# Picking the experts' input rows with products on TensorE instead of a store and indirect gathers

## The reference, cut to what matters

```python
glog = h @ w_rg + b_rg;  gprob = softmax(glog);  g_idx = argmax(glog);  g_w = max(gprob)     # 4 groups
elog = h @ w_re + b_re                                                                       # 8 experts per group
ev, ei = top_k(elog[g_idx], 2);  ew = softmax(ev)                                            # 2 of 8
combine[expert] = g_w * ew                                                                   # zero for all others
y += sum_e  (silu(h @ w_gate[e]) * (h @ w_up[e]) * combine[e]) @ w_down[e]                   # 32 experts
```

## Time and profile before

| | us |
|---|---|
| three runs | 734.08, 734.78, 737.99 |
| median | 734.78 |
| profiled execution: span from first to last instruction | 733.4 |
| its own time | not listed apart; the median is 1.4 over the span |

### The profile page before, as it was taken

One profiled execution on the slowest core, in us unless ns is written; L12 is line 12 of the kernel. 1 busy time (PEld: TensorE's weight loads), 2 busy tenths in 40 slices (PEclk: granted clock), 3 DMA queues, 4 the chain that ended last, 5 costly groups with the idle time before them and its releaser, 6 DMA issues.

```text
span 733.4 us, 13507 instructions
## 1 busy us (share of the span) xinstructions
PE 637.2 (87%) x4935; PEld 450.3 (61%) x4935; DVE 281.4 (38%) x1551; ACT 149.3 (20%) x425; POOL 103.4 (14%) x137
## 2 busy tenths in 40 slices
PE   6999999799999989999998999638997995768674
PEld 4888888687888767743535877436653554444431
DVE  3003845988878976400000222535233221110103
ACT  3333323233326222200010000211100110101013
POOL 1456206320100324000000000011100110000001
PEclk9999999999999999999999999858998998999996
DMA  9938997999998999769999699668999999999871
GB/s 308 291 116 296 365 370 251 328 352 381 348 337 311 391 351 363 301 246 349 410 409 360 224 423 388 266 214 311 351 391 402 372 389 397 388 390 416 365 264 61
DMA packets 94901, 242.86 MB, mean 331 GB/s; under 512 B 8834, under 2 KB 54530, under 8 KB 86514
## 3 DMA queue, kind: packets, MB, share of 16 engines
q1 hardware_dynamic: 58050, 193.51, 69.9%
q10 hardware_dynamic: 31200, 31.39, 12.9%
q0 software_dynamic: 5584, 17.08, 6.9%
HBM read 234.88 MB, written 9.11 MB: 333 GB/s over the span
## 4 chain that ended last, share of the span: by engine, by line
PE 65%; DMA 19%; DVE 9%; SPq 3%; issue 2%; ACT 1%; ACTq 0%; DVEq 0%; POOLq 0%
PE zps L913 40%; PE nps L1195 5%; PE nps L1071 4%; DMA ring_all<-in_w_up 3%; DMA headT<-in_w_up 3%; DMA kall<-in_w_up 3%; DVE kall L1385 3%; DMA ring_all<-in_w_ret_o 3%; PE zps L1218 2%; DMA zret<-in_w_up 2%; PE nps L884 2%; DMA hT<-in_w_down 2%; PE zps L884 1%; PE zps L1184 1%; SPq L453 1%
## 5 line engine op out<-in xcount | busy, mean ns | idle before, releaser
L913 PE MATMUL zps<-hT,ring_all 128*128 128x264 f32 x1152 | 273.5, 393 | 1.6 <-DVE hT L1564 1.0
L913 PEld LDWEIGHTS zps<-hT,ring_all 128*128 128x128 f32 x1152 | 217.6, 193 | 44.9 <-issue 4.2
L1385 DVE CUSTOM_DVE_ANT_0 kall<-kall,qb 128x128 f32<-128x128 f32 x512 | 129.2, 318 | 62.5 <-DMA kall<-in_cache_k 60.0
L606 POOL DMA_INDIRECT rows_b<-h_rows,tidx_i x16 | 15.0, 938 | 343.7 <-DVEq L1652 193.5
L913 PE MATMUL zps<-headT,ring_all 128*128 128x264 f32 x256 | 58.5, 388 | 3.6 <-DMA ring_all<-in_w_ret_o 2.2
L913 PEld LDWEIGHTS zps<-headT,ring_all 128*128 128x128 f32 x256 | 48.2, 190 | 14.7 <-issue 4.8
L1071 PE MATMUL nps<-ring_all,zret 128*64 128x512 f32 x224 | 51.5, 599 | 2.6 <-DMA ring_all<-in_cache_v 2.6
L1726 DVE TENSOR_TENSOR qdT<-qdT,nps 128x64 f32<-128x64 f32 x32 | 7.1, 221 | 101.7 <-ACT qdT L820 101.2
L1385 DVE DVE_READ_ACCUMULATOR2_ANT scores<- 128x1 f32 x512 | 40.5, 79 | 0.0
L1551 DVE TENSOR_TENSOR hT<-zps,zatt 128x264 f32<-128x264 f32 x8 | 3.5, 432 | 92.7 <-PE zps L913 92.6
L820 ACT ACTIVATE qdT<-nps 128x64 f32<-128x64 f32 x32 | 7.1, 223 | 144.5 <-PE nps L1195 144.5
(11 more groups left out here) (374 smaller groups left out, 805.8 us busy)
## 6 DMA issues: line engine op xcount, KB each, us to landing
kall<-in_cache_k SPq DMA_DIRECT2D x64, 512.0 KB, 6.7
ring_all<-in_cache_v SPq DMA_DIRECT2D x56, 512.0 KB, 7.7
ring_all<-in_w_in ACTq DMA_DIRECT2D x26, 1024.0 KB, 9.7
ring_all<-in_w_gate SPq DMA_DIRECT2D x10, 1024.0 KB, 21.5
ring_all<-in_w_up SPq DMA_DIRECT2D x10, 1024.0 KB, 24.4
ring_all<-in_w_down SPq DMA_DIRECT2D x8, 1024.0 KB, 12.7
ring_all<-in_w_in SPq DMA_DIRECT2D x6, 1024.0 KB, 13.4
kall<-in_w_gate SPq DMA_DIRECT2D x5, 1024.0 KB, 16.9
```

Source lines behind the costliest of these rows:

```text
L606: pool.indirect_dma_start(out=rows, out_offset=None, in_=h2_rows, in_offset=bass.IndirectOffsetOnAxis(ap=col, axis=0), bounds_check=T - 1, ...
L913: mm = pe.matmul(zps[m % 2][:, 0:T], w[:, k, P * fb:P * (fb + 1)], rhs[:, k, :], start=(k == 0), stop=(k == KT - 1))
L1385: ins = v.tensor_tensor_reduce(kh, kh, qb[b % 2][:, P * h:P * (h + 1)], 1.0, 0.0, ALU.mult, ALU.add, scores[:, pg, AH * b + h:AH * b + h + 1])
```

## The change

The rows of a quad (4 experts, 128 slots) are now picked by products. DVE builds `chosen`, for each of the three row tiles a matrix tokens x 128 slots that holds the token's inverse root where the token has the slot and 0 elsewhere (`choose`, two instructions of 128x384). TensorE multiplies, for each of 8 feature blocks and each of 3 row tiles, the residual rows `xs[0:r, t, k:DM:KT]` (weights, every eighth column) with `chosen` (128 columns moving), adding up over the row tiles. A quad has two halves of 4 blocks, 12 products each; `quad_x_copy` takes each half with the gain into `xgT`, which now holds a whole quad. The store of `h2_rows`, the row table, the index conversion, the gathers and the transposes are gone. The residual of the samples, which grows during the stage, is moved to a copy on partitions 32 to 39, because `xs` must stay as it was.

```diff
-            sp.wait_ge(h2_out, 48)
+            sp.wait_ge(h2_root, 1)
             down_in(5, 5)
@@ GpSimd
-            pool.wait_ge(h2_out, 48)
-            pool.wait_ge(t_idx, 1)
-            def gather(par, rows, col):
-                pool.indirect_dma_start(out=rows, out_offset=None, in_=h2_rows,
...
-            for p in range(NPAIR):
-                if p >= 2:
-                    pool.wait_ge(e_T, p - 1)
-                gather(p % 2, xg[p % 2], tidx_i[0:2 * CAP, p:p + 1])
@@ ScalarE
-            for t, r in enumerate(ROWS):
-                link(act.activation(h2n[t][0:r, :], xs[0:r, t, :], ACT.Copy, scale=st[0:r, 9 + t:10 + t]))
-                act.dma_start(h2_rows[P * t:P * t + r, :], h2n[t][0:r, :]).then_inc(h2_out, 16)
+            copy(ysam, xs[0:NB, 2, :]).then_inc(y_kept, 1)
@@ TensorE
-            pe.wait_ge(t_lhs, 2)
-            row_table(bps[:, 768:768 + NE], onA, onB)
+            def chosen_rows(out, k, slots):
+                for t, r in enumerate(ROWS):
+                    mm = pe.matmul(out, xs[0:r, t, k:DM:KT], chosen[0:r, t, 0:slots], start=(t == 0), stop=(t == 2))
+                return mm
+            def quad_x(bank, q, half):
+                pe.wait_ge(e_chosen, q + 1)
+                for k in range(HK):
+                    mm = chosen_rows(bank[:, P * k:P * (k + 1)], HK * half + k, P)
+                mm.then_inc(e_T, 1)
+            for half in range(2):
+                quad_x(zps[half], 0, half)
...
+            def next_quad_x(q, half):
+                pe.wait_ge(e_Tc, 2 * q + half)
+                if q >= 2 or half == 1:
+                    pe.wait_ge(e_pickTc, q - 1 + half)
+                quad_x(zps[0], q, half)
...
             for e in range(NE):
                 expert_gate_up(e)
-                if e % 2 == 0 and e // 2 + 1 < NPAIR:
-                    pair_x(e // 2 + 1)
+                if e % 2 == 1 and e // 4 + 1 < NQUAD:
+                    next_quad_x(e // 4 + 1, e % 4 // 2)
                 if e >= 5 and e % 4 in (1, 2):
                     quad_down(e // 4 - 1, e % 4 - 1)
                 h_tr(e % 2, e + 1)
...
-                if e == 4:
-                    tile_rows()
@@ VectorE
+            def choose(q, pos):
+                if q >= 1:
+                    v.wait_ge(e_T, 2 * q)
+                out = chosen[:, :, :].rearrange("p t (e c) -> p t e c", e=4)
+                link(at_slots(out, q, pos))
+                v.tensor_tensor(out, out, rE[:, :, 4 * q:4 * (q + 1)].unsqueeze(3).to_broadcast([P, 3, 4, CAP]),
+                                ALU.mult).then_inc(e_chosen, 1)
             v.wait_ge(t_pos, 1)
...
+            choose(0, mps[:, 0:3 * NE].rearrange("p (t e) -> p t e", t=3))
...
-            x_copy(0, 1, 2 * CAP)
+            for half in range(2):
+                quad_x_copy(zps[half], 0, half)
+            token_weights()
+            v.wait_ge(y_kept, 1)
             for e in range(NE):
                 hidden(e % 2, e + 1)
-                if e % 2 == 0 and e // 2 + 1 < NPAIR:
-                    x_copy((e // 2 + 1) % 2, e // 2 + 2, 2 * CAP)
-                if e == 0:
-                    token_weights()
+                if e // 4 + 1 < NQUAD:
+                    if e % 4 == 0:
+                        choose(e // 4 + 1, posE)
+                    if e % 2 == 1:
+                        quad_x_copy(zps[0], e // 4 + 1, e % 4 // 2)
                 if e % 4 == 1:
                     pick_rows(e // 4)
...
-                if e == 5:
-                    tile_rows()
```

More of the change, by code:

```diff
@@ L39 @@
 TILES = P // CAP
-NPAIR = NE // 2
+HK = KT // 2
 NQUAD = NE // 4
@@ L56 @@
            ("kdec", RH), ("rope", 2 * T), ("diag", NB * NB), ("own", AH), ("spread", NB * AH), ("edge", EDGES), ("slot", CAP),
-           ("order", NE), ("val", 6), ("tile", XT), ("before", 16), ("after", 16)]
+           ("order", NE), ("tile", XT), ("before", 16), ("after", 16)]
 COL, _at = {}, 0
@@ L264, in build @@
         v_soon = [kall[:, 0:2048], kall[:, 2048:4096], zdec_all[:, 0:2048], zdec_all[:, 2048:4096]]
-        xg = [rows_b[2 * CAP * i:2 * CAP * (i + 1), :] for i in range(2)]
         ysb = rows_a
+        at_s = slice(32, 32 + NB)
+        ysam = xs[at_s, 2, :]
         scores_f = scores[:, :, :].rearrange("p a b -> p (a b)")
@@ L275, in build @@
             down_w[i] = ring[(g + 2) % RING]
-        xgT = [gain[:, 512 * i:512 * (i + 1)] for i in range(2)]
+        xgT = [buf[:, :].rearrange("p (k s) -> p k s", k=KT) for buf in (gain, rows_b)]
+        chosen = sb("chosen", [P, 3, P])
         acT = [scores_f[:, 256 * i:256 * (i + 1)] for i in range(2)]
@@ L871, in _ @@
             act.wait_ge(f_gained, 1)
-            act.activation(fsam, fbuf[1][0:NB, :], ACT.Copy, scale=st[0:NB, 11:12]).then_inc(o_x[2], 1)
+            act.activation(fsam, fbuf[1][at_s, :], ACT.Copy, scale=st[at_s, 11:12]).then_inc(o_x[2], 1)
             act.wait_ge(o_x[2], 1)
@@ L1164, in tile_base @@
             def tile_base():
[L1165 removed]
+                pe.wait_ge(t_lhs, 2)
                 pe.matmul(mps[:, 640:640 + NE], xcnt_b, upper[0:NE, 0:NE], start=True, stop=True)
                 pe.matmul(mps[:, 704:705], xcnt_b, ones[0:NE, 0:1], start=True, stop=True).then_inc(t_pos, 1)
[L1169 to L1185 removed]
             def gate_up(par, x, b, x_copied, landed):
@@ L1236, in sample_rows @@
             def sample_rows(bank, q, half, rows):
-                pe.matmul(bank[0:NB, :], pickT[q % 2][0:rows, S:T], ysb[0:rows, 512 * half:512 * (half + 1)],
-                          start=True, stop=True).then_inc(e_S, 1)
+                pe.matmul(bank[at_s, :], pickT[q % 2][0:rows, S:T], ysb[0:rows, 512 * half:512 * (half + 1)],
+                          start=True, stop=True, tile_position=(0, 32)).then_inc(e_S, 1)
             y_n, s_n = [0], [0]
@@ L1681, in tile_tables @@
                 link(v.tensor_copy(xexp[:, XT:XT + 1], mps[0:1, 704:705]))
+                v.sem_inc(t_read, 1)
+                for k in range(2):
+                    ins = v.tensor_tensor(prod[:, 3 * k:3 * k + 3, :], oh12[:, 3 * k:3 * k + 3, :], posE, ALU.mult)
+                link(ins)
+                link(v.tensor_reduce(pos6, prod, AX.X, ALU.add))
                 link(v.tensor_tensor(prod, oh12, xbase.unsqueeze(1).to_broadcast([P, 6, NE]), ALU.mult))
@@ L1708, in tile_experts, with x_copy, quad_x_copy @@
                 v.sem_inc(t_exp, 1)
-            def tile_rows():
-                v.wait_ge(t_tabs, 2)
-                d, w = rows_from(bps[:, 768:768 + XT], slice(0, P), NE, NT)
-                link(v.tensor_scalar(w, d, T - 0.5, -float(T), ALU.is_gt, ALU.mult))
-                link(v.tensor_tensor(tidx_i[:, NE:NT], w, d, ALU.add))
-                v.sem_inc(t_idx, 1)
-            def x_copy(par, n, rows):
-                v.wait_ge(e_T, n)
-                v.tensor_tensor(xgT[par].rearrange("p (k s) -> p k s", k=KT)[:, :, 0:rows],
-                                zps[0][:, :].rearrange("p (k s) -> p k s", k=KT)[:, :, 0:rows],
-                                fT[:, :].unsqueeze(2).to_broadcast([P, KT, rows]), ALU.mult).then_inc(e_Tc, 1)
+            def x_copy(out, bank, ks, n):
+                v.wait_ge(e_T, n)
+                shape = [P, ks.stop - ks.start, out.shape[-1]]
+                v.tensor_tensor(out[:, ks, :], bank.rearrange("p (k s) -> p k s", k=shape[1]),
+                                fT[:, ks].unsqueeze(2).to_broadcast(shape), ALU.mult).then_inc(e_Tc, 1)
+            def quad_x_copy(bank, q, half):
+                x_copy(xgT[q % 2], bank[:, :], slice(HK * half, HK * (half + 1)), 2 * q + half + 1)
             def hidden(par, n):
```

138 lines of the change are left out of this document (44 added, 94 removed).

## The result

| | before | after |
|---|---|---|
| median of runs, us | 734.87 (734.08 to 737.99) | 824.59 (822.68 to 826.24, 4 runs) |
| ratio, 95% interval | | 1.1218 (1.1190 to 1.1246) |
| span of the profiled execution, us | 733.4 | 823.0 |
| mean granted TensorE clock | 0.950 | 0.899 |

A forecast was written before the change was run, and what follows sets the result against it. It took TensorE's (with DVE's) race against DMA to bound the stage up to 579 us, then DMA. Quad 2's downs 15 us later, then 43.0 MB at 416 GB/s, gave +5.5 us on 733.4 and, with 1.4, 740.3 us; range 732 to 749.

The forecast's parts named there:

- I take 0.13 ... 3.1 us per half quad: TensorE's row-picking products: 0.13 us per instruction with strided weights, 24 instructions or 3.1 us per half quad at full clock.
- The high end: Upper bound for one strided product instruction: 0.166 us with the stride's 0.054 added whole, or 0.136 if the load alone limits.
- This is the gain, 8 us: Weights queue behind 579 us: without gathers its 43.68 MB take 105 us at 416 GB/s instead of 113.
- The start: a gain of 2.7 us: Start of the expert stage: gate/up 0 done at 493.9 instead of 496.6, a gain of 2.7 us.
- the first 4.5 us: First quad's 48 product instructions: some 4.5 us at 1.2 GHz, then 28 at 0.13 us, 8.1 us in all.
- Later waits stay covered: Waits after quad 2's downs (put at 594.4) stay hidden: quad 3's come 25 us later, and 12 MiB last 30.
- The prediction's own test for a quad: Later quads: TensorE's time from one quad's downs to the next, 25 us, against 30 us of DMA for 12 MiB.
- rival (c): Half-quad products: stride free, clock as before; quad 2's downs at 590.9, weights in at 697.0, 736.8 us; chance 0.25.
- the rule weighed: TensorE's clock: transposes don't count as busy as products do, so products would hold 2.4 GHz more often; no term of the sum.
- (a): TensorE in the expert stage: clock stays up and stride is free, half quads of 2.7 us, 729.9 us; chance 0.07.
- (b): Weight loads: the downs' waits never bind, 71 MiB without a gap at 416 GB/s, 715 us; chance 0.04.
- (d): Half-quad products: the stride costs all of its 0.054 us, half quads of 4.0 us, 747.2 us; chance 0.22.

The follow-up runs named there:

- padded_step8: The padded kernel with every eighth column of the reordered rows as weights again (other features): 773.1 us, ratio 1.0540.
- padded: The permuted kernel with the third tile's products over all 128 rows, rows 8 to 127 of `chosen` being zeros: 739.0 us, ratio 1.0060.
- permuted: The changed kernel with residual rows copied once by ScalarE, feature-reordered, so the products' weights are contiguous and the sums the same: 759.4 us, ratio 1.0344.
- after: The changed kernel itself, with weights at a step of eight and 8 rows in the third tile: 824.6 us, ratio 1.1218.
- grouped: The changed kernel with the four 8-row products of each half quad put behind its eight 128-row ones, step of eight kept: 796.1 us, ratio 1.0838.
- no_gathers: The kernel before the change without its last 14 gathers, transposes reading rows of pairs 0 and 1 again: 722.4 us, ratio 0.9838.
- contiguous: The changed kernel with 128 adjacent columns as weights instead of every eighth (other features): 754.5 us, ratio 1.0266.
- step2: The changed kernel with every second column as weights instead of every eighth (other features): 757.3 us, ratio 1.0308.
- rows32: The padded kernel with the third tile's products over 32 rows instead of 128: 761.8 us, ratio 1.0386.
- padded_step4: The padded kernel with every fourth column as weights (other features): 771.1 us, ratio 1.0513.
- permuted_two: The permuted kernel without the products of the third row tile, the 8 sample rows: 730.9 us, ratio 0.9950.
- two_tiles: The changed kernel without the products of the third row tile (the 8 sample rows), step of eight kept: 745.3 us, ratio 1.0145.

## Why the prediction was wrong

**The failed step is the cost of a half quad: "I take 0.13 ... 3.1 us per half quad", with 4.0 at most.** It measured 7.64. From the runs: contiguous and unmixed 2.95 us (starts 0.11 apart, and the tail of the last); the step of eight adds 3.0 (padded_step8 against padded); changes of the row count add 1.3 without the step (permuted against padded) and 1.5 to 1.7 with it (after against grouped and padded_step8). Two things were wrong in it:

- The high end came from transposes, 0.136 us for a strided one. A product's instruction with strided weights costs 0.24, and its load lasts 0.33 us (L1121 above) where the transposes' loads last 0.20 (first row below). Transposes of 64 rows and f32 products are not the same form; no row of before held the step and the form together, so that end should have been left open. (Its sum, 0.11 + 0.054, is also 0.164 and not 0.166.) The Trainium skill's sentence on lines of 16 bytes (SBUF — State Buffer, cited above) was the rule to weigh against this change: by it every element of the strided load opens a new line.
- The stall was not thought of at all, though the kernel before has rows that look like it, where 128-row and 8-row transposes alternate (groups of weight loads by form; the last columns are idle us before them and what ended it):

```profile
L1184 PEld LDWEIGHTS zps<-cst,rows_b 64*128 64x128 f32 x64 | 7.7, 201 | 1.8 <-issue 1.8
...
L884 PEld LDWEIGHTS zps<-cst,xs 128*128 128x128 f32 x24 | 2.8, 158 | 13.2 <-DMA cst<-shape_constants 6.7 <-issue 6.5
L884 PEld LDWEIGHTS zps<-cst,xs 8*128 8x128 f32 x12 | 1.8, 149 | 2.6 <-issue 2.6
```

In the last row, 2.6 us of idle time before 12 loads is 0.22 each, close to the 0.2 of a changed count in permuted: the row was there to be priced. That it is the same stall is a likeness of numbers; no run changed these transposes.

**"This is the gain, 8 us"** was too small as well: the gathers cost 12.7 us (no_gathers), because what they took before 579 us was put at nothing. This error pulls the other way, and the half quads' outweighs it by far.

**"The start: a gain of 2.7 us"** was a loss of 8.1 (504.7 against 496.6). The first quad took 16.3 us, not 8.1, and the clock did not rise behind the first 4.5 us: it was 0.50 until 500, and gate/up 0 and 1 took 3.64 us each.

**"Later waits stay covered" fell with it.** Quad 2's downs came at 647.5, not 594.4. The prediction's own test for a quad, 30 us of DMA against TensorE's time, was right; with 7.6 us half quads it reads 37.6 against 30.2. In padded, where a half quad costs 2.95, quad 2's downs are at 595.44 and the rest is the DMA's, as the prediction had it: 17.6 us later than in no_gathers (577.85), and 739.0 - 722.4 = 16.6 us longer in all. So the picture of the path was sound. At half quads of 2.7, in rival (c), it gave 590.9, 4.5 us too early.

**The account from padded to the changed kernel,** 85.9 us between the profiled executions (823.0 and 737.1), from the windows behind 480 us, of the changed kernel and then of padded (columns as in the earlier trace rows):

```profile
480.00:823.00 343.00, 312.18 (x2960) 206.96 (x2960) 65.45 (x197) 32.83 (x98) 2.35 (x1) 0.77 0.60 240
```
```profile
480.00:737.00 257.00, 213.40 (x2960) 141.84 (x2960) 66.20 (x202) 35.99 (x100) 2.34 (x1) 0.93 0.80 321
```

From 480 us on TensorE is busy 98.8 us longer and idle 12.8 us less. 8.2 us of the latter are waits for gate/up weights, which padded has behind 659 us and the changed kernel has not at all. Of the 98.8, the first quad is 16.3 - 7.3 = 9.0, and the fourteen half quads are 14 x (7.75 - 2.95) = 67. The other 22 or so are the same instructions as in padded at a lower clock, 0.77 against 0.93 in these windows: gate/up was busy for 80.8 us instead of 72.9, the down products for 42.2 instead of 33.4, the adds into the accumulators for 41.1 instead of 33.6. Behind a half quad the groups of down products start 0.85 us apart (715.13, 715.98), behind gate/up 0.43 (683.11, 683.54).

On the rule weighed, of transposes and the clock: products in place of transposes did not hold 2.4 GHz in the changed kernel (0.77 from 480 us on); in padded, where they neither alternate nor have a step, the windows from 520 to 560 and from 580 to 680 show a granted clock of 1.00. No run separates the transposes from the rest, so the rule itself stays untested. Rivals (a), (b) and (c) are refuted; (d) named one of the two causes and, with half quads of 4.0, a fifth of the miss (0.9 of 4.5 us over the forecast's 3.1).

## What to carry to other kernels

Before a gather is turned into products, price one product in its exact form: its step in bytes, its type, and the row counts of its neighbours. Where a ragged last tile alternates with full ones, fill it with zeros to the full row count or put all its products together; where a strided operand is used many times, reorder it once. And compare, stage by stage, the new time of the engine with the DMA time of the same work: a cost that passes it is paid in full from there on.

## What was not expected of the hardware

- An f32 weight load at a step of four or eight elements makes an instruction cost 0.23 to 0.25 us instead of 0.11 at full clock. At 1.2 GHz the step costs much less on top: 16 strided ones took 4.21 us in grouped's first quad (482.96, granted clock 0.52 in that window) and 4.07 later, while pairs of contiguous ones start 0.42 apart in padded's first quad (485.46, 485.88) and 0.22 later.
- A change between 128 rows and 8 or 32 rows costs 0.2 us at 2.4 GHz (0.42 instead of 0.22 between the starts of pairs of loads), and more at 1.2: a block of three products took 1.87 us in permuted's first quad and 1.06 later.
- The clock can stay down under a busy engine. In 480 to 500 us the granted clock was 0.50 in all kernels whose products alternate in row count (after, contiguous, step2, permuted, rows32), with PE busy for 17.5 us of it in the changed kernel; where they don't alternate it was 0.78 (padded_step8), 0.75 (padded_step4), 0.79 (padded, permuted_two), 0.66 (two_tiles) and 0.52 in grouped. The step alone didn't keep it down. What did so in grouped, whose first quad has only three changes, stays open. Later, from 560 to 720 us, it was 0.98 with the alternation alone (contiguous, permuted), 0.99 with the step alone (padded_step8) and 0.81 with both (after).
- Fourteen gathers of 1.9 MB in all cost 12.7 us beside a full queue: 4.6 us are their own bytes at 416 GB/s, the rest is rate that the weights' queue lost beside them.
